# Attention bias spread over the rows by two heads at a time, the first U pair's mix read two steps later, and the values of odd softmax blocks one step later

## The chip, the cores and the metric

The kernel runs on one core of a Trainium2 chip. The time is that of one execution on the device, in microseconds; 910.57 us is the median of three runs (908.77 to 911.44). Of the core's engines the text names TensorE (PE), VectorE (DVE), ScalarE (ACT), GpSimd (POOL) and SyncE (SP), which issues most of the DMAs. Every engine works through its own list of instructions in order and waits on semaphores where it needs another's result. DMAs issued on one engine share that engine's queue.

## The reference

One block of a decoder with two token mixers side by side, for a sequence of 1024 rows and a width of 1024, all float32:

```
h      = rms_norm(x, pre_norm)
q,k,v,gate_a,u,v_b,gate_b,mg_a,mg_b = split(h @ w_in)
o_a    = sliding_window_attention(q, k, v, sinks, rel_bias)   # 16 q heads, 2 kv heads, window 128
y_a    = (o_a * silu(gate_a)) @ w_branch_a
o_b    = gelu(u) * (tril(w_s) @ layer_norm(gelu(v_b)) + b_s)  # chunks of 128, 8 groups
y_b    = (o_b * silu(gate_b)) @ w_branch_b
merged = sigmoid(mg_a) * y_a + sigmoid(mg_b) * y_b
x      = x + rms_norm(merged @ w_out, post_norm)
```

In the attention a row t sees the keys t-127 to t and one sink per head. A bias that depends on the head and on the distance between row and key alone is added to the scores before the softmax:

```
scores = einsum('bnqhgd,bnkhd->bnhgqk', qb, kb) * HEAD_DIM ** -0.5
scores = where(mask, scores + bias, NEG_INF)
m      = maximum(max(scores), sink);  p = exp(scores - m)
probs  = p / (sum(p) + exp(sink - m));  out = probs @ vb
```

## The kernel before

**Products.** A float32 operand is kept as two parts, high and low, and each product is three passes of fp32r matmuls (high by high, high by low, low by high). Over that lies a scheme of seven products for the four quarters of a result. One product is 12 matmuls of 128x512 on PE (`product`, L1079); sums of operands before it and of results behind it (`c_11`, `c_12`, `c_21`, `c22` and so on) are made by DVE, ACT and GpSimd.

**Stages.** Up to about 115 us the kernel computes the V half of the gMLP branch: tiles t of 128 rows, each with loads of x rows, a layer norm, and the spatial mix, whose result goes to `mix_d` in DRAM. Then k and v are projected. Then come 24 pairs n, each with seven steps s, one product per step. Pairs 0 to 15 alternate between Q pairs (q and `gate_a` of two heads) and M pairs (the merge gates); from pair `FIRST_U` = 16 on they are U pairs, which compute u and `gate_b` and multiply u by the mixed values. Last come three square products, by `w_branch_a`, `w_branch_b` and `w_out`, from about 672 us to the end.

**Attention beside the products.** The attention of a head pair p is laid over the products of the pairs: each step k of a head pair does a piece of it, in the middle of a product, after six of its 12 matmuls. A head pair starts every 14 steps and runs on for up to six steps into the next. It has eight blocks of 128 rows, whose scores come at k = 0, 1, 3, 4, 6, 7, 9 and 10 (`BLOCK_AT`). `blocks_at(k, lag)` gives the blocks whose turn it is, so many steps behind their scores; `even_at` and `odd_at(k, lag)` give the even ones, or the odd ones for which 3j + lag == k.

- An odd block's probabilities are transposed on PE (`transpose_p`, L1046, at k = 3j + 3), and DVE splits them into `pt_pack` (L2126, L2127).
- An even block's are transposed in small squares on DVE (L2146) and rearranged through DRAM: SP stores them at k = 3j + 2 (`prob_away`, L651, to `prob_d`) and loads them in four pieces at 3j + 3 (`prob_back`, L660, to `turned_in`). ACT and DVE split them (L1588, L2151).
- GpSimd masks the part of the previous block (`pt_prev`, L1857). PE multiplies by the values (`values`, L1067): even blocks at k = 3j + 7, odd ones at 3j + 5.
- Before that, DVE adds the bias and takes the maximum (L2137), ACT takes the exponential (L1570), DVE the reciprocal of the sum (L2117), and ACT scales (L1578).

Each engine has a function `attend(p, k)` with its part of a step, and a loop that calls it after the other work of step s of pair n; on DVE that other work is `after(n, s)`.

**The bias.** Its 384 values per head stand in DRAM (`bias_d`, 16 x 384). ACT issues one DMA in tile t = 5 that copies each head's row 128 times, to `skew_d` (16 x 128 x 384, 3 MB):

```
act.dma_start(skew_d[:, :, :], bass.AP(bias_d, 0,
    [[BIAS_ROW, N_HEADS], [0, P], [1, BIAS_ROW]])).then_inc(bias_out, 16)
```

From there `load_bias(p)` on SP reads two heads along a skewed pattern into `bias_t` (L644), for the next head pair at k = 11.

**The first U pair.** `u_mix(n)` on DVE multiplies a tile `ub` that SP loads from `mix_d` (L707) by a column of gains and adds a constant (L2172); `u_mul` (L2182) multiplies a half of u by it. In U pairs before the last they stand at steps 3 and 4. In pair 16 the last head pair's attention still runs beside them.

**x rows.** For a tile t, SP loads rows of x into `x_both` (L499, L506). DVE transposes them in squares (L1965) on the way to the h tile, of which `mv` (L1982) is a part that PE waits for (L872).

Of the kernel before, what the change touches and what calls it, by code (L numbers as in the profile page):

```python
# [5 lines left out]
P = 128  # L6
# [3 lines left out]
N_HEADS = D_MODEL // HEAD_DIM  # L10
# [9 lines left out]
HEAD_PAIRS = N_HEADS // 2  # L20
# [121 lines left out]
def build(nc, x, rel_bias, pre_norm, post_norm, w_in, sinks, sgu_ln_g, sgu_ln_b,  # L142
# [26 lines left out]
    with ExitStack() as ctx:  # L169
# [217 lines left out]
        def neg_w(blk, h):  # L387

            c = (blk % 2 * 2 + h) * SINK_W
            return neg_s[:, c:c + SINK_W]  # L390

        bmat = ub[:, 3072:4096]


# [101 lines left out]
        def _(sp):  # L496
# [140 lines left out]
                return out[0, bass.ds(t * P, P), cols]  # L637

            def load_bias(p):
                if p == 0:  # L640
                    sp.wait_ge(bias_out, 32)
                else:
                    sp.wait_ge(scores_used, 8 * p)
                sp.dma_start(bias_t[:, :].rearrange("p (h j) -> p h j", h=2),  # L644
                             bass.AP(skew_d, p * (2 * P * BIAS_ROW) + (P - 1),
                                     [[BIAS_ROW - 1, P], [P * BIAS_ROW, 2], [1, 2 * P]])).then_inc(bias_in, 16)
# [16 lines left out]
            def attend(p, k):  # L663
                for blk in even_at(k, 2):
                    prob_away(4 * p + blk // 2)
                for blk in even_at(k, 3):
                    prob_back(4 * p + blk // 2)
                if k == 11 and p + 1 < HEAD_PAIRS:
                    load_bias(p + 1)
                if k in (13, 19):  # L670
# [193 lines left out]
        def _(pe):  # L864
# [204 lines left out]
                ins.then_inc(values_ok, 1)  # L1069

            def attend(p, k):
                for blk in odd_at(k, 5) + even_at(k, 7):
                    values(p, blk)
                for blk in odd_at(k, 3):
                    transpose_p(p, blk)
                for blk in blocks_at(k, 0):
                    scores(p, blk)
# [133 lines left out]
        def _(act):  # L1211
# [107 lines left out]
            for t in range(2, NT):  # L1319
                if 2 < t < NT - 1:  # L1320
                    square_x(t + 1)
                if t == 5:
                    act.wait_ge(bias_out, 16)
                    act.dma_start(skew_d[:, :, :], bass.AP(bias_d, 0, [[BIAS_ROW, N_HEADS], [0, P], [1, BIAS_ROW]])).then_inc(bias_out, 16)
                if t == 2:
                    act.wait_ge(mix_done, 1)
                    vn_split(1)
# [596 lines left out]
        def _(dve):  # L1924
# [519 lines left out]
            def after(n, s):  # L2444
# [19 lines left out]
                if s == 3:  # L2464
                    if n and kind(n - 1) == "Q":
                        gate_mul(n - 1, 1)
                    c_22(n)
                    if kind(n) == "U" and n < PAIRS - 1:
                        u_mix(n)
                if s == 4:  # L2470
                    if n == PAIRS - 1:
                        c_11(n)
                        left_lo_square(0)
                    if kind(n) == "U":
                        u_mul(n, 0)
                    if n == PAIRS - 4:
                        right_lo_square(0)
                if s == 6:
                    if kind(n) == "Q":
                        q_lo(n, 1)  # L2480
# [120 lines left out]
```

## Time and profile before

| | us |
|---|---|
| median of three runs | 910.57 |
| lowest and highest | 908.77, 911.44 |
| the profiled execution, its own time | 908.92 |
| its span in the profile | 907.2 |
| PE busy | 894.8 |
| DVE busy | 671.5 |
| ACT busy | 500.9 |
| POOL busy | 498.2 |

The span runs from the first to the last instruction that the profile records; the execution's own time has 1.7 us around it. Shares of busy time are averages over the stages. A timeline row gives the start, the duration, the engine, the line and the operation with its output and inputs and, in brackets, how long the engine had been idle and which engine's result ended that. SPq and ACTq are the issues of DMAs on SP and ACT; their duration is that of the issue and not of the transfer. Ends of matmuls are modelled.

### The profile page before, as it was taken

The page shows a single profiled execution, that of the slowest core. Times are in us where ns is not written, and L with a number is a line of the kernel's source. Part 1 is how long each engine was busy: PE and PEld are TensorE (multiplying, and loading weights), DVE is VectorE, ACT ScalarE, POOL GpSimd, SP SyncE. Part 2 cuts the span into 40 slices and gives each one's busy share as a digit, 9 for nine tenths or more (in the row PEclk, how much of TensorE's full clock was granted, in tenths as well). Part 3 has the DMA queues.
Part 4 walks back from the last instruction along what each step waited for, and adds up shares of the span by engine and source line. Part 5 has one row for each costly group of instructions (what it writes and reads, how often), then busy time and mean ns, then how long its engine had stood idle before and what let it go on. Part 6 is the DMA issues. An engine that isn't in the chain of part 4 may idle for free.

```text
span 907.2 us, 12749 instructions
## 1 busy us (share of the span) xinstructions
PE 894.8 (99%) x4268; PEld 746.9 (82%) x4268; DVE 671.5 (74%) x1167; ACT 500.9 (55%) x982; POOL 498.2 (55%) x395
## 2 busy tenths in 40 slices
PE   9999999999999999999999989999999999999997
PEld 7888788888888888888888868888888888888886
DVE  6766695576666666757576669688689878989968
ACT  6554254775767676666767664334443434534563
POOL 3564235777787777787869636445542252043236
PEclk9999999999999999999999999999999999999999
DMA  8788764433434346534343443533289550435004
GB/s 311 194 201 241 240 209 105 136 104 86 134 88 127 95 117 163 150 105 117 102 116 103 116 146 105 186 117 123 62 292 334 185 209 1 139 114 211 1 1 185
DMA packets 170512, 130.90 MB, mean 144 GB/s; under 512 B 58552, under 2 KB 139472, under 8 KB 170320
## 3 DMA queue, kind: packets, MB, share of 16 engines
q1 hardware_dynamic: 168208, 126.66, 45.7%
q10 hardware_dynamic: 2240, 3.43, 1.2%
q8 instruction: 34, 0.56, 0.3%
q14 instruction: 30, 0.25, 0.1%
HBM read 93.87 MB, written 39.35 MB: 147 GB/s over the span
## 4 chain that ended last, share of the span: by engine, by line
PE 84%; DVE 5%; ACT 4%; issue 3%; SPq 2%; DMA 1%; POOL 0%; DVEq 0%; POOLq 0%; ACTq 0%
PE acc L1019 42%; PE acc L1200 11%; PE ps_m L1200 7%; PE ps_t L1200 7%; PE acc L872 7%; PE ps_t L1036 2%; PE acc L962 2%; PE ps_m L1067 2%; SPq L506 1%; ACT prob L1570 1%; DVE neg_s L2137 1%; DVE pt_pack L2151 1%; ACT prob L1578 1%; DVE ps_t L2134 1%; PE ps_t L1046 1%
## 5 line engine op out<-in xcount | busy, mean ns | idle before, releaser
L1019 PE MATMUL acc<-mv,w_hi 128*128 128x512 f32 x1344 | 353.8, 392 | 0.0
L1019 PEld LDWEIGHTS acc<-mv,w_hi 128*128 128x128 f32 x1344 | 244.8, 188 | 44.9
L1019 PE MATMUL acc<-mv,w_lo 128*128 128x512 f32 x672 | 182.0, 393 | 0.0
L1813 POOL TENSOR_TENSOR w_lo<-sums,w_hi 128x1024 fp32r<-128x1024 f32 x48 | 118.0, 2460 | 73.1 <-ACT w_hi L1366 48.9
L1019 PEld LDWEIGHTS acc<-mv,w_lo 128*128 128x128 f32 x672 | 126.7, 189 | 28.6
L1813 POOL TENSOR_TENSOR w_lo<-raw,w_hi 128x1024 fp32r<-128x1024 f32 (+1 forms) x48 | 95.2, 1984 | 40.1 <-ACT w_hi L1359 32.6
L1570 ACT ACTIVATE prob<-neg_s,neg_max 128x129 f32<-128x129 f32 x128 | 50.5, 396 | 89.7 <-DVE neg_max L2137 89.6
L1200 PE MATMUL acc<-right,left 128*128 128x512 f32 x432 | 98.7, 389 | 0.0
L1200 PEld LDWEIGHTS acc<-right,left 128*128 128x128 f32 x432 | 81.0, 188 | 17.2 <-DVE left L2203 0.4
L2151 DVE TENSOR_TENSOR pt_pack<-turned_in,pt_pack 128x256 fp32r<-128x256 f32 x32 | 43.6, 1362 | 42.5 <-ACT pt_pack L1588 42.5
L1857 POOL TENSOR_SCALAR_AFFINE_SELECT pt_prev<-pt_pack 128x512 fp32r<-128x512 f32 x64 | 40.8, 638 | 58.6 <-DVE pt_pack L2127 39.8
L872 PE MATMUL acc<-mv 128*128 128x512 f32 x288 | 69.3, 394 | 0.2 <-ACT mv L1233 0.2
L1200 PE MATMUL ps_t<-right,left 128*128 128x512 f32 x288 | 67.2, 389 | 0.0
L1200 PE MATMUL ps_m<-right,left 128*128 128x512 f32 x288 | 67.2, 389 | 0.0
L1200 PEld LDWEIGHTS ps_t<-right,left 128*128 128x128 f32 x288 | 54.1, 188 | 11.2
L1200 PEld LDWEIGHTS ps_m<-right,left 128*128 128x128 f32 x288 | 54.1, 188 | 11.2
L872 PEld LDWEIGHTS acc<-mv 128*128 128x128 f32 x288 | 53.2, 188 | 11.7 <-ACT mv L1233 0.4
L1578 ACT ACTIVATE prob<-prob,inv_den 128x128 f32<-128x128 f32 x128 | 44.1, 392 | 22.0 <-DVE inv_den L2117 22.0
L2137 DVE CUSTOM_DVE_ANT_0 neg_s<-ps_t,bias_t,sink_b 128x128 f32<-128x128 f32 x128 | 39.9, 350 | 4.5 <-PE ps_t L1036 2.4
L1819 POOL TENSOR_TENSOR left<-w_a,left 128x1024 fp32r<-128x1024 f32 x7 | 18.4, 2644 | 37.4 <-ACT left L1507 37.4
L1819 POOL TENSOR_TENSOR left<-s_buf,left 128x1024 fp32r<-128x1024 f32 x6 | 15.2, 2556 | 43.0 <-ACT left L1507 43.0
L1819 POOL TENSOR_TENSOR left<-w_b,left 128x1024 fp32r<-128x1024 f32 x6 | 16.4, 2751 | 38.3 <-ACT left L1507 38.3
(286 smaller groups left out, 1688.0 us busy)
## 6 DMA issues: line engine op xcount, KB each, us to landing
raw<-in_w_in SPq DMA_DIRECT2D x56, 512.0 KB, 4.5
ht_d<-sums SPq DMA_DIRECT2D x8, 512.0 KB, 4.9
mix_d<-mix_b SPq DMA_DIRECT2D x8, 512.0 KB, 4.0
prob_d<-prob SPq DMA_DIRECT2D x32, 128.0 KB, 2.2
turned_in<-prob_d SPq DMA_DIRECT2D x128, 32.0 KB, 2.2
ga_d<-gate SPq DMA_DIRECT2D x16, 256.0 KB, 4.1
tb<-tb_d SPq DMA_DIRECT2D x4, 1024.0 KB, 5.1
ub<-mix_d SPq DMA_DIRECT2D x7, 512.0 KB, 3.4
```

Of the source, the lines that this page charges most:

```text
L872: ins = nc.tensor.matmul(acc[b][:, hf * HALF:(hf + 1) * HALF], left, right, start=(m < 2), stop=(m >= 46), skip_group_check=True)
L962: ins = nc.tensor.matmul(acc[b][:, hf * HALF:(hf + 1) * HALF], (w_lo if x == 2 else w_hi)[:, w], right, start=(m < 2), stop=(m >= 46), ski ...
L1019: ins = nc.tensor.matmul(bank, (w_lo if y == 2 else w_hi)[:, left + k * P:left + (k + 1) * P], right[:, (OPW if y == 1 else 0) + k * HALF: ...
L1036: ins = nc.tensor.matmul(ps_s[:, h * 256 + lo:(h + 1) * 256], q_st[h][:, blk * P:(blk + 1) * P], kbuf[:, kc + lo:kc + 256], start=a, stop= ...
L1200: ins = nc.tensor.matmul(bank, l[:, c:c + P], r[:, (OPW if y == 1 else 0) + k * HALF:(OPW if y == 1 else 0) + (k + 1) * HALF], start=(m == ...
L1570: ins = nc.scalar.activation(prob_w(s, h, SINK_W), neg_w(blk, h), ACT.Exp, scale=-1.0, bias=neg_max[:, head(blk, h)], accum_out=row_sum[:, ...
L1578: ins = nc.scalar.activation(w, w, ACT.Copy, scale=inv_den[:, head(blk, h)])
L1813: nc.gpsimd.tensor_tensor(w_lo[:, c], src, w_hi[:, c].bitcast(f32), ALU.subtract).then_inc(wlo_ok, 1)
L1819: ins = nc.gpsimd.tensor_tensor(left[f % 2][:, OPW:2 * OPW][:, c], left_src(f // 7, ORDER[f % 7])[:, c], left[f % 2][:, c].bitcast(f32), A ...
L1857: nc.gpsimd.affine_select(out=pt_prev[blk % 2][:, :].rearrange("p (y q) -> p y q", y=4), in_=pt_pack[blk % 2][:, :].rearrange("p (y q) -> ...
L2137: ins = nc.vector.tensor_tensor_reduce(out=neg_w(blk, h)[:, 0:P], in0=ps_s[:, h * 256 + P:(h + 1) * 256], in1=bias_t[:, bias:bias + P], sc ...
L2151: nc.vector.tensor_tensor(pack[:, 256:512], turned_in[:, :], pack[:, 0:256].bitcast(f32), ALU.subtract).then_inc(ptl_ok, 1)
```

## The change

Three edits:

1. `skew(p)` gives the source and the destination of the spread of two heads. ACT issues only `skew(0)` in tile t = 5. SP issues `skew(p + 1)` at k = 7 of head pair p, seven times in all. `load_bias(p)` waits for `bias_out` of its own piece, beside `scores_used`.
2. In pair 16 alone `u_mix` and `u_mul(n, 0)` stand on DVE in step 5 and not in steps 3 and 4. The other U pairs keep them.
3. The values of odd blocks stand on PE at k = 3j + 6.

```diff
--- before.py
+++ after.py
@@ -388,6 +388,11 @@
 
             c = (blk % 2 * 2 + h) * SINK_W
             return neg_s[:, c:c + SINK_W]
+
+        def skew(p):
+
+            return (skew_d[2 * p:2 * p + 2, :, :],
+                    bass.AP(bias_d, 2 * p * BIAS_ROW, [[BIAS_ROW, 2], [0, P], [1, BIAS_ROW]]))
 
         bmat = ub[:, 3072:4096]
 
@@ -637,9 +642,8 @@
                 return out[0, bass.ds(t * P, P), cols]
 
             def load_bias(p):
-                if p == 0:
-                    sp.wait_ge(bias_out, 32)
-                else:
+                sp.wait_ge(bias_out, 32 + 16 * p)
+                if p:
                     sp.wait_ge(scores_used, 8 * p)
                 sp.dma_start(bias_t[:, :].rearrange("p (h j) -> p h j", h=2),
                              bass.AP(skew_d, p * (2 * P * BIAS_ROW) + (P - 1),
@@ -665,6 +669,8 @@
                     prob_away(4 * p + blk // 2)
                 for blk in even_at(k, 3):
                     prob_back(4 * p + blk // 2)
+                if k == 7 and p + 1 < HEAD_PAIRS:
+                    sp.dma_start(*skew(p + 1)).then_inc(bias_out, 16)
                 if k == 11 and p + 1 < HEAD_PAIRS:
                     load_bias(p + 1)
                 if k in (13, 19):
@@ -1069,7 +1075,7 @@
                 ins.then_inc(values_ok, 1)
 
             def attend(p, k):
-                for blk in odd_at(k, 5) + even_at(k, 7):
+                for blk in odd_at(k, 6) + even_at(k, 7):
                     values(p, blk)
                 for blk in odd_at(k, 3):
                     transpose_p(p, blk)
@@ -1321,7 +1327,7 @@
                     square_x(t + 1)
                 if t == 5:
                     act.wait_ge(bias_out, 16)
-                    act.dma_start(skew_d[:, :, :], bass.AP(bias_d, 0, [[BIAS_ROW, N_HEADS], [0, P], [1, BIAS_ROW]])).then_inc(bias_out, 16)
+                    act.dma_start(*skew(0)).then_inc(bias_out, 16)
                 if t == 2:
                     act.wait_ge(mix_done, 1)
                     vn_split(1)
@@ -2465,16 +2471,19 @@
                     if n and kind(n - 1) == "Q":
                         gate_mul(n - 1, 1)
                     c_22(n)
-                    if kind(n) == "U" and n < PAIRS - 1:
+                    if FIRST_U < n < PAIRS - 1:
                         u_mix(n)
                 if s == 4:
                     if n == PAIRS - 1:
                         c_11(n)
                         left_lo_square(0)
-                    if kind(n) == "U":
+                    if n > FIRST_U:
                         u_mul(n, 0)
                     if n == PAIRS - 4:
                         right_lo_square(0)
+                if s == 5 and n == FIRST_U:
+                    u_mix(n)
+                    u_mul(n, 0)
                 if s == 6:
                     if kind(n) == "Q":
                         q_lo(n, 1)
```

Lines below the new function stand five or six lines further down in the changed kernel: L651 becomes L655, L1067 becomes L1073, L2172 becomes L2178.

On SP, in the second head pair around its step 7: `raw` is the buffer of the next weight load, `ta_d` and `tb_d` are gates of M pairs. Before:

```order
L527 DMA raw<-in_w_in 128x8x128 [waits wlo_ok,sum_ok]
L651 DMA prob_d<-prob 256x1x128 [waits turn_ok]
L685 DMA tb_d<-ev 128x512 [waits mt_ok]
L660 DMA turned_in<-prob_d 32x8x32 [waits ptl_ok,prob_out]
L660 DMA turned_in<-prob_d 32x8x32 x3
L651 DMA prob_d<-prob 256x1x128 [waits turn_ok]
L644 DMA bias_t<-skew_d 128x2x256 [waits scores_used]
L660 DMA turned_in<-prob_d 32x8x32 [waits ptl_ok,prob_out]
```

And now:

```order
L532 DMA raw<-in_w_in 128x8x128 [waits wlo_ok,sum_ok]
L673 DMA skew_d<-bias_d 256x1x384
L655 DMA prob_d<-prob 256x1x128 [waits turn_ok]
L691 DMA tb_d<-ev 128x512 [waits mt_ok]
L664 DMA turned_in<-prob_d 32x8x32 [waits ptl_ok,prob_out]
L664 DMA turned_in<-prob_d 32x8x32 x3
L655 DMA prob_d<-prob 256x1x128 [waits turn_ok]
L648 DMA bias_t<-skew_d 128x2x256 [waits scores_used,bias_out]
L664 DMA turned_in<-prob_d 32x8x32 [waits ptl_ok,prob_out]
```

The spread of the next two heads stands behind a weight load and ahead of the third even block's store and loads. `load_bias` waits for it six rows further down.

On DVE, in steps 3 to 6 of pair 16, from the sum `c22` on (`ub` is the tile from `mix_d`, `bmat_in` and `mix_in0` say that its loads are there). Before:

```order
L2078 TENSOR_TENSOR c<-acc,c 128x512 [waits ev_ok]
L2172 SCALAR_TENSOR_TENSOR ub<-ub,g_col 128x1024 [waits bmat_in,mix_in0]
L2117 RECIPROCAL inv_den<-row_sum 128x2 [waits exp_ok,mm_ok]
L2151 TENSOR_TENSOR pt_pack<-turned_in,pt_pack 128x256 [waits turn_hi]
L2158 TENSOR_TENSOR o_tmp<-ps_m,o_tmp 64x256 [waits otmp_ok]
L2159 TENSOR_TENSOR o_tmp<-ps_m,o_tmp 64x256 [waits dve_own]
L2182 TENSOR_TENSOR ub<-ub,ev 128x512 [waits gu_ok]
L2126 CAST pt_pack<-ps_t 128x256 [waits values_ok,pt_done]
L2127 TENSOR_TENSOR pt_pack<-ps_t,pt_pack 128x256 [waits dve_own]
L2182 TENSOR_TENSOR ub<-ub,c 128x512 [waits gu_ok]
L2083 TENSOR_TENSOR ev<-acc,ev 128x512 [waits ev_ok,prod]
```

And now:

```order
L2084 TENSOR_TENSOR c<-acc,c 128x512 [waits ev_ok]
L2123 RECIPROCAL inv_den<-row_sum 128x2 [waits exp_ok]
L2157 TENSOR_TENSOR pt_pack<-turned_in,pt_pack 128x256 [waits turn_hi]
L2164 TENSOR_TENSOR o_tmp<-ps_m,o_tmp 64x256 [waits otmp_ok]
L2165 TENSOR_TENSOR o_tmp<-ps_m,o_tmp 64x256 [waits dve_own]
L2132 CAST pt_pack<-ps_t 128x256 [waits values_ok,pt_done]
L2133 TENSOR_TENSOR pt_pack<-ps_t,pt_pack 128x256 [waits dve_own]
L2178 SCALAR_TENSOR_TENSOR ub<-ub,g_col 128x1024 [waits bmat_in,mix_in0]
L2188 TENSOR_TENSOR ub<-ub,ev 128x512 [waits gu_ok,mm_ok]
L2188 TENSOR_TENSOR ub<-ub,c 128x512 [waits gu_ok]
L2089 TENSOR_TENSOR ev<-acc,ev 128x512 [waits ev_ok,prod]
```

The mix has moved from ahead of the reciprocal to behind the split of the last odd block, and the first multiplication stands right behind it.

On PE, in the second head pair, the values of an odd block (`ps_m` is the result, `oadd_ok` says that its bank is free) and the next transposes (`ps_t`). Before:

```order
L1067 MATMUL ps_m<-pt_pack,v_st 128x2x128 [waits oadd_ok,pt_ok]
L1067 MATMUL ps_m<-pt_pack,v_st 128x2x128
L1067 MATMUL ps_m<-pt_prev,v_st 128x2x128 x2
L1019 MATMUL acc<-mv,w_hi 128x512 x2
L1019 MATMUL acc<-mv,w_lo 128x512 [waits wlo_ok]
L1019 MATMUL acc<-mv,w_lo 128x512 x3
L1019 MATMUL acc<-mv,w_hi 128x512 [waits c22_ok,whi_ok]
L1019 MATMUL acc<-mv,w_hi 128x512 x5
L1046 MATMUL ps_t<-ident,prob 128x128 [waits ptl_ok,prob_ok]
L1046 MATMUL ps_t<-ident,prob 128x128
L1036 MATMUL ps_t<-k_hi,q_st 128x256 [waits scores_used,ql_ok]
L1036 MATMUL ps_t<-k_lo,q_st 128x256
```

And now:

```order
L1025 MATMUL acc<-mv,w_hi 128x512 x7
L1025 MATMUL acc<-mv,w_lo 128x512 [waits wlo_ok]
L1025 MATMUL acc<-mv,w_lo 128x512 x3
L1025 MATMUL acc<-mv,w_hi 128x512 [waits c22_ok,whi_ok]
L1025 MATMUL acc<-mv,w_hi 128x512 x5
L1073 MATMUL ps_m<-pt_pack,v_st 128x2x128 [waits oadd_ok,pt_ok]
L1073 MATMUL ps_m<-pt_pack,v_st 128x2x128
L1073 MATMUL ps_m<-pt_prev,v_st 128x2x128 x2
L1052 MATMUL ps_t<-ident,prob 128x128 [waits ptl_ok,prob_ok]
L1052 MATMUL ps_t<-ident,prob 128x128
L1042 MATMUL ps_t<-k_hi,q_st 128x256 [waits scores_used,ql_ok]
```

The four matmuls of the values have moved behind the rest of one product and the first half of the next, to just before the transposes of the next odd block.

## Rows read from the trace of the kernel before

**Rows 1.** Page, section 1: busy us, share of the span, instructions, by engine
```profile
PE 894.8 (99%) x4268; PEld 746.9 (82%) x4268; DVE 671.5 (74%) x1167; ACT 500.9 (55%) x982; POOL 498.2 (55%) x395
```
**Rows 2.** Waits of PE: line and what it waited for, us, times, longest us
```profile
PE ps_t L1046 <- ACT prob L1578: 3.4, 1, 3.4
...
PE acc L872 <- DVE mv L1982: 1.1, 1, 1.1
PE ps_t L1036 <- DVE neg_max L2137: 0.8, 1, 0.8
```
**Rows 3.** Timeline of PE: start us, us, operation, [idle before, releaser]
```profile
534.96 0.69 PE L1046 MATMUL ps_t<-ident,prob 128*128 128x128 f32 x2 [3.38 <-ACT prob L1578]
535.30 1.20 PE L1019 MATMUL acc<-mv,w_hi 128*128 128x512 f32 x2
...
537.88 0.85 PE L1019 MATMUL acc<-mv,w_hi 128*128 128x512 f32 x3
```
**Rows 4.** Windows: us, busy PE to POOL, PEclk, DMA share, GB/s
```profile
535.30:537.90 2.60, 2.60 (x9) 2.08 (x8) 2.14 (x5) 2.56 (x5) 0.64 (x1) 0.53 0.19 44
537.90:548.00 10.10, 10.10 (x50) 8.46 (x49) 8.49 (x10) 6.38 (x10) 7.52 (x6) 1.00 0.32 88
```
**Rows 5.** Timeline of DVE, ACT and SP's queue, 527 to 535 us
```profile
529.00 0.69 DVE L2078 TENSOR_TENSOR c<-acc,c 128x512 f32<-128x512 f32 x1 [1.01 <-ACT c L1418]
532.70 1.28 DVE L2172 SCALAR_TENSOR_TENSOR ub<-ub,g_col 128x1024 f32<-128x1024 f32 x1 [3.00 <-DMA ub<-mix_d]
...
534.22 0.69 ACT L1578 ACTIVATE prob<-prob,inv_den 128x128 f32<-128x128 f32 x2 [5.25 <-DVE inv_den L2117]
...
527.97 0.91 SPq L707 DMA_DIRECT2D ub<-mix_d  x2
```
**Rows 6.** Timeline of DVE at 93 us
```profile
93.21 1.25 DVE L1965 STREAM_TRANSPOSE sums<-x_both 128x1024 f32<-128x1024 f32 x1 [4.30 <-DMA x_both<-in_x]
```
**Rows 7.** Timeline of SP's queue, 60 to 95 us, and a DMA issue
```profile
63.95 5.75 SPq L506 DMA_DIRECT2D x_both<-in_x  x4
...
77.44 12.60 SPq L506 DMA_DIRECT2D x_both<-in_x  x4
...
skew_d<-bias_d ACTq DMA_DIRECT2D x1, 3072.0 KB, 15.8
```
**Rows 8.** DMA queues from 75 to 77 us: packets, MB, share of 16 engines
```profile
q10 hardware_dynamic: 493, 0.76, 106.7%
```
**Rows 9.** Timeline of SP's queue, second head pair
```profile
233.74 0.39 SPq L527 DMA_DIRECT2D raw<-in_w_in  x1
235.20 0.56 SPq L651 DMA_DIRECT2D prob_d<-prob  x1
...
239.71 3.38 SPq L660 DMA_DIRECT2D turned_in<-prob_d  x4
```
**Rows 10.** Landing: weight load (KB, us), the store L651, the loads L660
```profile
raw<-in_w_in SPq DMA_DIRECT2D x1, 512.0 KB, 4.3
...
DMA to landing us min/median/max: 3.2/3.2/3.2
...
DMA to landing us min/median/max: 2.0/2.2/3.0
```
**Rows 11.** Timeline of ACT, DVE and PE, 248 to 255 us
```profile
248.08 0.40 ACT L1588 ACTIVATE pt_pack<-turned_in 128x256 fp32r<-128x256 f32 x1
...
248.51 0.90 DVE L2151 TENSOR_TENSOR pt_pack<-turned_in,pt_pack 128x256 fp32r<-128x256 f32 x1 [1.07 <-ACT pt_pack L1588]
...
254.85 0.48 DVE L2151 TENSOR_TENSOR pt_pack<-turned_in,pt_pack 128x256 fp32r<-128x256 f32 x1
...
252.17 0.40 PE L1067 MATMUL ps_m<-pt_pack,v_st 128*128 128x256 f32 x2
```
**Rows 12.** Timeline of GpSimd (POOL) at 241 us, PE at 246 us
```profile
241.41 0.64 POOL L1857 TENSOR_SCALAR_AFFINE_SELECT pt_prev<-pt_pack 128x512 fp32r<-128x512 f32 x1 [1.06 <-DVE pt_pack L2127]
...
245.95 0.40 PE L1067 MATMUL ps_m<-pt_pack,v_st 128*128 128x256 f32 x2
```

## The prediction

> **What bounds the kernel now.** I read the busy shares first: TensorE (PE) is busy for 894.8 us of the 907.2 us span [rows 1], so time can be won only where PE stands still. Next come PE's own waits [rows 2]. After the start there are three: 3.38 us (3.4 in the row) for the scaled probabilities from ACT, 1.1 us for DVE's `mv`, and 0.8 us for DVE's `neg_max`. Everything else that DVE, ACT, GpSimd and the queues do lies beside matmuls. A change can give back at most these waits and what they trail behind them, while whatever it delays by more than its cover becomes a new PE wait. So for each part I ask: which of the three waits does it touch, and whose cover does it use up?
>
> **The first U pair's mix.** PE is free at 534.96 - 3.38 = 531.58 and waits until 534.96 [rows 3]. The wait has a tail: the six matmuls that follow run from 535.30 to 537.88, 2.58 us, and the granted clock of that stretch is 0.53, the lower of the two levels (1.2 GHz), after PE had stood still; the stretch after it shows 1.00 [rows 3, 4]. At the full clock the six take half of it, 1.29, so the tail is 1.29 us and the whole 3.38 + 1.29 = 4.7 us. The cause stands on DVE: it sums `c22` until 529.69, then sits 3.00 us in `u_mix` until the load of `mix_d`, issued at 527.97, has landed, and the mix takes 1.28 [rows 5]. Behind it in DVE's order is the reciprocal of the last softmax block; ACT's scaling (0.69 us) begins 0.24 us after the mix ends, and PE's transposes wait for that.
>
> With `u_mix` moved behind step 5's copies, the reciprocal follows `c22`: ACT scales from 529.69 + 0.24 = 529.93 to 530.62, 0.96 us before PE is free. The wait and its tail go. What is late next? The load lands at 532.7 as before, since its issue waits for the last mask and not for the mix. By then DVE has done the steps in front of it. It mixes until 534.0, multiplies (`u_mul`, moved with it), and its first result for PE is the sum `c_21`, which needs product 4 of this pair, two products further on. Nothing on PE waits for the mixed tile. The mix, 1.28 us, and `u_mul` are hidden by those two products; if they were not, their cost would be their own length. Term: **-4.7 us**.
>
> **The bias spread, first piece.** The wait for `mv` is the h tile of the last row block: DVE stood 4.30 us for the x rows [rows 6]. SP's four issues for these rows take 12.60 us, where the four of an earlier block took 5.75: they were held up [rows 7]. At that time the whole 3 MB spread (`skew_d`, landing after 15.8 us) filled the DMA engines: from 75 to 77 us all packets are its own, 493 of them at 106.7% of 16 engines [rows 7, 8]. The change leaves an eighth of it here, 2 heads of 16. PE needs the x rows 1.1 us sooner, out of a delay of several us. Bounds: 0 if some engines still carry as much as before, 1.1 if the way is clear. I take 0.8, nearer the upper end, since the piece leaves most engines free and ends earlier. Term: **-0.8 us**.
>
> **The bias spread, seven pieces on SP.** This is the cost. Each piece is issued on SP at step 7 of a head pair, between a 512 KB weight load and the store of the third even block's probabilities (`prob_away`). The issue itself, some 0.6 us, is hidden: SP waits for turned probabilities after it. What counts is how long a piece occupies the DMA engines, t. No row shows a spread of two heads. Ends: 15.8 / 8 = 2.0 us if it runs on all engines like the whole, 15.8 us if an eighth of the rows takes as long as all. Between them lies the rate: 493 packets in 2 us on 16 engines are 65 ns each [rows 8]. Before, 16 heads of 128 rows went over 16 engines, 128 rows each. The new source pattern begins with 2 heads, not 16. If a head stays on one engine, a piece is again 128 rows per engine: 128 x 65 ns = **8.3 us**. I take this value, since its load per engine is that of the measured spread.
>
> *The Trainium skill, "DMA: Bandwidth & Descriptors", section "Why a DMA increments its semaphore by 16 and not by 1", says that a DMA of this kind uses the largest number of engines, up to 16, that divides the outermost dimension above 1 of both patterns: here 2. No row here shows it. By it the piece has 8.3 us and the sum is the forecast; a piece spread over 16 engines would give rival 2.*
>
> Now the chain behind it, in the second pair. The weight load is issued at 233.74 and lands 4.3 later, at 238.0 [rows 9, 10]. The piece begins on its engines as that ends, about 237.5, and holds them until 237.5 + 8.3 = 245.8. The store, issued at 235.20 and landing 3.2 later, at 238.4, now lands at about 246.1. SP's four loads of turned blocks (`prob_back`) wait for that: 246.1 and not 239.71. Their issues take 2.5 us (3.38 here, one was slow), the last starts at 248.0 and lands 2.2 later [rows 10], at 250.2. ACT copies them 0.40, DVE 0.48 to 0.90 [rows 11], GpSimd 0.64 [rows 12]: ready at 251.8 to 252.3 with 0.1 for the hand-offs. PE wants them at 252.17 [rows 11]. So the cover (1.3 us in front of the loads, 3.5 us before ACT's 248.08, 2.0 us before PE) is just used up: PE waits 0 to 0.2 us, and from there one us of t costs one us in each of seven pairs. I take 0.2 x 7. The new wait of `load_bias` for its piece is covered: it stands four steps on, about 13 us, against 8.3 + 2. Behind it in SP's order stand the last block's `prob_back` loads, about 2 us late, which ACT needs at the time it has them today; its later idle time takes that up. Term: **+1.4 us**.
>
> **The values of odd blocks, one step later.** GpSimd's `pt_prev` for such a block is done at 242.05, and PE takes it at 245.95 [rows 12]: these values never wait, so a step more of room gives nothing. Nor does it cost: the four matmuls move from before one product and a half to just before the next transposes and scores, which then stand where they stood. The next odd block's copy waits for them and for the transposes directly behind, and those come last anyway. Term: **0**.
>
> **Sum**: -4.7 - 0.8 + 1.4 = -4.1 us. The profiled execution took 908.92 us; the median of the runs, 910.57, stands 1.65 above it. 908.92 - 4.1 = 904.8, and 906.5 for a median.
>
> **The rivals.** About 0.3%, 2.7 us, is what a measurement of this kernel can tell from no change.
> 1. *The pieces are too long: slower.* If a packet costs more when two engines carry all of them, or something queues in front, PE waits at the values of the third even block of seven pairs for t - 8.1 each. The gains are 5.5, so it decides from t = 8.1 + 5.5 / 7 = 8.9 us, 8% above my value. At t = 9.5 it is 7 x 1.4 = 9.8: +4.3, 914.9. For it: no cover is left in [rows 9 to 11]. Against: the 65 ns were taken with all 16 engines copying, and two should not be worse off. Chance 0.17; the end at 15.8 us (7 x 7.7) gets almost none of it.
> 2. *The pieces are short.* If they use all engines, t is 2.0 us, no chain is late, and the x rows are free: -4.7 - 1.1 = -5.8, 904.8. Against: the source pattern. Chance 0.13.
> 3. *The gain is given back: no change.* With t = 8.6 the pieces cost 3.5, or DVE, without PE's standstill to catch up in, lets PE wait about 2 us in the next U pairs: -2.0, 908.6. For it: DVE is busy at 74% [rows 1] and is given two operations later. Chance 0.25.
>
> The forecast itself has 0.45. Faster: 0.45 + 0.13 = 0.58; same 0.25; slower 0.17. The range goes from 903.5 (rival 2 and a fast set of runs) to 914.0 (t about 9.4); above it lies the far part of rival 1, near 0.1, below it 0.05.
>
> **What the profile after would show.** Right: PE's 3.4 us wait for ACT and the stretch at 0.53 gone; DVE's wait for `mix_d` at most short; seven pieces that land some 10 to 12 us after issue; `prob_away` of the third block landing after about 10 us and not 3; ACT idle before the third copy of `turned_in`. The forecast is wrong if PE shows seven waits of 1 us or more at L1073 (the values), if the pieces land after 4 us (rival 2), or if the wait for `mv` stays at 1.1 us (the term of 0.8).

## The result and the profile after

The changed kernel took 917.69 us (median of five, 914.92 to 919.85) where the kernel before took 909.84 (median of five on the same chip): a ratio of 1.0084, interval 1.0063 to 1.0105. It is slower by 7.9 us; the forecast was 906.5 with a range up to 914.0. The profiled execution took 916.38 us, 7.46 more than the one before.

The page's busy shares, to be read against [rows 1]:

```profile
PE 898.6 (98%) x4268; PEld 748.6 (82%) x4268; DVE 667.9 (73%) x1167; ACT 500.5 (55%) x982; POOL 501.1 (55%) x395
```

No engine has more instructions. PE is busy for 3.8 us more and idle for 3.6 more. PE's waits are the next view; each row names the line, what it waited for, us in all, times and the longest:

```profile
PE ps_m L1073 <- POOL pt_prev L1863: 5.9, 6, 1.6
PE ps_t L1042 <- issue: 2.0, 1, 2.0
PE acc L1096 <- DVE before L2496: 1.1, 1, 1.1
PE ps_t L1042 <- DVE neg_max L2143: 0.9, 1, 0.9
```

Against [rows 2], the wait for ACT (3.4) is gone, and so is the one for `mv` (1.1). In their place stand six waits at L1073, the values, and one at L1042 that names no engine. PE's timeline gives each its place:

```profile
251.15 0.50 PE L1073 MATMUL ps_m<-pt_pack,v_st 128*128 128x256 f32 x2 [0.29 <-POOL pt_prev L1863]
...
299.52 0.50 PE L1073 MATMUL ps_m<-pt_pack,v_st 128*128 128x256 f32 x2 [0.76 <-POOL pt_prev L1863]
...
348.44 0.51 PE L1073 MATMUL ps_m<-pt_pack,v_st 128*128 128x256 f32 x2 [1.31 <-POOL pt_prev L1863]
353.89 0.30 PE L1042 MATMUL ps_t<-k_hi,q_st 128*128 128x128 f32 x1 [1.96 <-issue]
...
400.18 0.51 PE L1073 MATMUL ps_m<-pt_pack,v_st 128*128 128x256 f32 x2 [1.05 <-POOL pt_prev L1863]
...
449.33 0.50 PE L1073 MATMUL ps_m<-pt_pack,v_st 128*128 128x256 f32 x2 [1.56 <-POOL pt_prev L1863]
...
497.89 0.50 PE L1073 MATMUL ps_m<-pt_pack,v_st 128*128 128x256 f32 x2 [0.95 <-POOL pt_prev L1863]
```

One per head pair from the second to the seventh: the third even block, the one behind a piece of the spread. The head pair's chain begins on SP's queue. The second head pair, to be read against [rows 9]:

```profile
232.37 0.39 SPq L532 DMA_DIRECT2D raw<-in_w_in  x1
232.81 0.64 SPq L673 DMA_DIRECT2D skew_d<-bias_d  x1
233.84 3.91 SPq L655 DMA_DIRECT2D prob_d<-prob  x1
237.79 0.93 SPq L691 DMA_DIRECT2D tb_d<-ev  x1
...
245.37 2.58 SPq L664 DMA_DIRECT2D turned_in<-prob_d  x4
```

The store (L655) follows the piece (L673), and the loads (L664) wait for it. They come 13.0 us after the weight load; before it was 239.71 - 233.74 = 5.97. The issue of the store alone holds SP for 3.91 us instead of 0.56. The store's landing, in this pair, and then the DMA queues from 241 to 244 us:

```profile
DMA to landing us min/median/max: 11.5/11.5/11.5
...
q1 hardware_dynamic: 98, 0.15, 13.3%
```

In those 3 us SP's queue moves 98 packets and keeps 13.3% of 16 engines busy, 2.1 of them: the piece runs on two engines. 49 packets each in 3 us are 61 ns a packet, so 128 of them take 7.8 us. By the Trainium skill, "DMA: Bandwidth & Descriptors", section "Why a DMA increments its semaphore by 16 and not by 1", the engines number the largest divisor up to 16 that the slowest dimensions of both patterns share, here 2; the trace agrees.

Where the time went is read from one more view: the start of PE's scores at step 3 of each head pair, minus the same start in the kernel before (each number is the difference of two rows of PE's timelines; the kernels' names are those of the experiments below).

| head pair | changed | pieces_alone | fourth_rows | rows96_long | pieces_on_act | rows_outermost | mix_and_values |
|---|---|---|---|---|---|---|---|
| 1st | -1.5 | -1.4 | -0.8 | -1.5 | -1.5 | -1.5 | -0.8 |
| 2nd | -1.6 | -1.4 | -0.6 | -1.7 | -1.7 | -1.6 | -0.9 |
| 3rd | -0.9 | -0.6 | 0.0 | -2.1 | -2.1 | -2.0 | -1.3 |
| 4th | +0.7 | +0.7 | +1.4 | -2.2 | -2.2 | -2.1 | -1.4 |
| 5th | +6.4 | +5.8 | +2.1 | -0.5 | -2.2 | -1.6 | -1.4 |
| 6th | +7.3 | +7.1 | +3.8 | -0.6 | -2.3 | -1.9 | -1.5 |
| 7th | +9.7 | +9.5 | +6.4 | -0.6 | -2.4 | -2.0 | -1.6 |
| 8th | +11.5 | +10.1 | +8.1 | -0.1 | -2.4 | -2.1 | -1.7 |
| its last scores | +12.1 | +10.5 | +8.8 | -0.1 | -2.5 | -2.1 | -1.7 |

The changed kernel enters the attention 1.5 us ahead (the x rows), loses 13.6 us up to its last scores, and ends 7.46 behind, so it wins 4.6 us after them (the mix).

The last column has no piece inside the attention, yet PE moves ahead by about 1 us there. That is edit 3; see values_alone below.

### The profile page after: what moved, and what is told of

It reads as the page before. It is cut to its first block, busy times and chain, and to the rows that moved or that the text cites. A ratio compares the mean times of both kernels' runs of the same rounds, so it can differ in the third digit from the quotient of the medians.

```text
span 914.6 us, 12763 instructions
## 1 busy us (share of the span) xinstructions
PE 898.6 (98%) x4268; PEld 748.6 (82%) x4268; DVE 667.9 (73%) x1167; ACT 500.5 (55%) x982; POOL 501.1 (55%) x395
## 4 chain that ended last, share of the span: by engine, by line
PE 60%; DMA 11%; DVE 9%; ACT 9%; issue 9%; SPq 2%; ACTq 0%; DVEq 0%; POOLq 0%; POOL 0%
PE acc L1025 19%; PE acc L1206 11%; PE acc L878 10%; DMA prob_d<-prob 9%; PE ps_m L1206 7%; PE ps_t L1206 7%; PE acc L968 2%; DMA turned_in<-prob_d 2%; SPq L664 2%; DVE neg_s L2143 2%; ACT prob L1584 2%; DVE gate L2109 2%; ACT prob L1576 2%; DVE ps_t L2140 1%; DVE pt_pack L2157 1%
## 5 line engine op out<-in xcount | busy, mean ns | idle before, releaser
L2157 DVE TENSOR_TENSOR pt_pack<-turned_in,pt_pack 128x256 fp32r<-128x256 f32 x32 | 38.1, 1191 | 67.3 <-ACT pt_pack L1594 67.3
L1863 POOL TENSOR_SCALAR_AFFINE_SELECT pt_prev<-pt_pack 128x512 fp32r<-128x512 f32 x64 | 44.3, 693 | 68.2 <-DVE pt_pack L2133 34.5
L1042 PE MATMUL ps_t<-k_hi,q_st 128*128 128x256 f32 (+1 forms) x128 | 35.6, 301 | 3.3 <-issue 2.0
```

What stands on the lines that cost most here:

```text
L1042: ins = nc.tensor.matmul(ps_s[:, h * 256 + lo:(h + 1) * 256], q_st[h][:, blk * P:(blk + 1) * P], kbuf[:, kc + lo:kc + 256], start=a, stop= ...
L1863: nc.gpsimd.affine_select(out=pt_prev[blk % 2][:, :].rearrange("p (y q) -> p y q", y=4), in_=pt_pack[blk % 2][:, :].rearrange("p (y q) -> ...
L2157: nc.vector.tensor_tensor(pack[:, 256:512], turned_in[:, :], pack[:, 0:256].bitcast(f32), ALU.subtract).then_inc(ptl_ok, 1)
```

## The experiments

Ratios are to the kernel before on the same chip, with their 95% interval.

| kernel | median us (range) | before | ratio |
|---|---|---|---|
| mix_alone | 904.33 (903.87 to 908.13) | 909.18 | 0.9958 (0.9944 to 0.9971) |
| values_alone | 908.70 (907.11 to 911.14) | 909.18 | 0.9993 (0.9982 to 1.0003) |
| pieces_alone | 920.08 (918.60 to 923.38) | 909.18 | 1.0125 (1.0107 to 1.0143) |
| rows_outermost | 902.12 (901.72 to 902.28) | 909.18 | 0.9920 (0.9906 to 0.9934) |
| fourth_rows | 912.80 (911.19 to 914.41) | 909.15 | 1.0036 (1.0023 to 1.0049) |
| pieces_on_act | 904.11 (901.89 to 904.76) | 909.15 | 0.9943 (0.9923 to 0.9963) |
| mix_and_values | 902.67 (902.31 to 902.78) | 909.15 | 0.9924 (0.9908 to 0.9940) |
| pieces_at_13 | 905.00 (903.85 to 905.79) | 909.15 | 0.9949 (0.9931 to 0.9967) |
| changed_again | 916.67 (916.03 to 917.11) | 909.33 | 1.0078 (1.0065 to 1.0091) |
| no_values | 917.73 (917.04 to 918.04) | 909.33 | 1.0089 (1.0076 to 1.0102) |
| rows96_long | 906.57 (904.29 to 908.15) | 909.33 | 0.9965 (0.9952 to 0.9979) |

### Each edit alone

**mix_alone**, against the kernel before:

```diff
-                    if kind(n) == "U" and n < PAIRS - 1:
+                    if FIRST_U < n < PAIRS - 1:
                         u_mix(n)
...
-                    if kind(n) == "U":
+                    if n > FIRST_U:
                         u_mul(n, 0)
...
+                if s == 5 and n == FIRST_U:
+                    u_mix(n)
+                    u_mul(n, 0)
```

> The kernel before with edit 2 alone (the mix and its first multiplication in step 5 of pair 16). Theory A (the loss comes from the pieces alone, and the mix gives what was forecast): PE's 3.38 us wait and the stretch at the lower clock are gone, 4.7 us less than before, about 905.1. Theory B (DVE catches up in PE's standstill, and loses it now): a new PE wait of about 2 us in pairs 17 to 19, about 907.

It is 4.85 us faster by the medians. The wait for ACT is gone and none has come in pairs 17 to 19: theory A. PE's waits:

```profile
PE acc L872 <- DVE mv L1982: 2.6, 1, 2.6
PE acc L1090 <- DVE before L2490: 1.1, 1, 1.1
PE ps_t L1036 <- DVE neg_max L2137: 0.8, 1, 0.8
```

The twelve runs of this kernel fall into two groups, seven at 903.9 to 904.4 us and five at 905.8 to 908.1. The profiled execution (907.66 us) is of the second and shows something else: with the spread whole, the wait for the x rows was 2.6 us here, 1.1 before [rows 2] and 0.2 in values_alone. It differs between executions.

**values_alone**, against the kernel before:

```diff
-                for blk in odd_at(k, 5) + even_at(k, 7):
+                for blk in odd_at(k, 6) + even_at(k, 7):
```

> The kernel before with edit 3 alone (the values of odd blocks at lag 6). Theory A: no change, 909.8, and the scores of the blocks at steps 4 to 7 keep their times. Theory B (the 0.3 to 0.5 us per head pair that the changed kernel loses between the scores of steps 4 and 7, ahead of the next piece, comes from the values): 2 to 3 us more, about 912.3.

Its interval holds 1: the times alone show no change. By the trace PE is 0.7 us ahead when the attention begins (the x rows, by chance) and 1.7 at its last scores, so it gains 1.0 us in between. The part between steps 4 and 7 is not lost here, so theory B falls; those losses belong to the pieces. Theory A wanted the scores at their old times, and that fails too. The gain is no chance of one trace: mix_and_values and pieces_on_act, which have edit 3 as well, gain 1.0 us in the same stretch, while mix_alone, which has not, stays 3.3 us behind the kernel before from the first scores to the last.

**pieces_alone** is the changed kernel with these two diffs undone, so that `skew`, its calls and the waits of `load_bias` are left:

```diff
-                for blk in odd_at(k, 6) + even_at(k, 7):
+                for blk in odd_at(k, 5) + even_at(k, 7):
...
-                    if FIRST_U < n < PAIRS - 1:
+                    if kind(n) == "U" and n < PAIRS - 1:
                         u_mix(n)
...
-                    if n > FIRST_U:
+                    if kind(n) == "U":
                         u_mul(n, 0)
...
-                if s == 5 and n == FIRST_U:
-                    u_mix(n)
-                    u_mul(n, 0)
```

> The kernel before with edit 1 alone (the first piece on ACT, seven on SP). Theory A: the six waits at the values, the wait for the k loads and the clock behind it stay, 1.5 us are won at the x rows: about +12, 922. Theory B (a part belongs to the values): +9.5, about 919.5.

10.9 us slower: nearer to B's number, but not for B's reason, since values_alone costs nothing. The table shows 11.9 us lost in the attention stage, 1.4 won before it. The pieces carry the whole loss.

### Why a piece is long

**rows_outermost** copies the same elements, with the pattern turned round:

```diff
-            return (skew_d[2 * p:2 * p + 2, :, :],
-                    bass.AP(bias_d, 2 * p * BIAS_ROW, [[BIAS_ROW, 2], [0, P], [1, BIAS_ROW]]))
+            return (skew_d[2 * p:2 * p + 2, :, :].rearrange("h r j -> r h j"),
+                    bass.AP(bias_d, 2 * p * BIAS_ROW, [[0, P], [BIAS_ROW, 2], [1, BIAS_ROW]]))
```

> The changed kernel with the same copy written with the 128 rows as the outermost dimension of source and destination, the heads behind them. Theory A (a piece is long because its outermost dimension is 2, so that two engines carry it): the pieces take about 2 us on all engines, the store lands after some 4 us, no wait at the values, none for k: the changed kernel less 12 to 13, about 904 to 905. Theory B (a piece of 128 rows of two heads is long whatever its order): as the changed kernel, 917.7.

902.12 us, 15.6 below the changed kernel and 7.1 below the one before: theory A, even below its number, and the lowest median of this study. SP's queue in the second head pair, and behind it the landing of that pair's store:

```profile
231.72 0.39 SPq L532 DMA_DIRECT2D raw<-in_w_in  x1
232.15 0.72 SPq L673 DMA_DIRECT2D skew_d<-bias_d  x1
233.18 0.56 SPq L655 DMA_DIRECT2D prob_d<-prob  x1
...
237.69 3.39 SPq L664 DMA_DIRECT2D turned_in<-prob_d  x4
...
DMA to landing us min/median/max: 4.5/4.5/4.5
```

The same 384 KB in the same place cost the loads nothing: 5.97 us after the weight load, as before. The piece itself landed 5.1 us after its issue. From 234 to 236 us SP's queue, with the piece and its neighbours in it, keeps all engines busy:

```profile
q1 hardware_dynamic: 885, 0.62, 106.1%
```

PE's waits in this kernel are two of about a microsecond that the kernel before has too, and one of 0.5 us at L1042. That one is for the key loads of the section on the fifth head pair below. They were issued as soon after the weight load as in the kernel before (13.1 us), but the last landed 7.3 us after its issue instead of 5.4. Why is not shown.

### What a long piece does to what stands behind it

**pieces_on_act** leaves the pieces long and issues them on ACT:

```diff
-                if k == 7 and p + 1 < HEAD_PAIRS:
-                    sp.dma_start(*skew(p + 1)).then_inc(bias_out, 16)
...
+                if k == 7 and p + 1 < HEAD_PAIRS:
+                    act.dma_start(*skew(p + 1)).then_inc(bias_out, 16)
```

> The changed kernel with the seven pieces issued on ACT at its step 7, so that they stand in another queue than the store. Theory A1 (the store waits because its packets stand behind the piece's in the same queue of two DMA engines): the store lands after 3 to 4 us, no waits at the values, 903 to 906. Theory A2 (the two engines are held, whatever the queue): as the changed kernel, 917. Between them, if the engines take turns between queues: the store lands 1 to 2 us later than before, 904 to 908.

904.11 us, and no wait at the values in the profiled execution. That one took 901.89 us; the other three took 903.93 to 904.76, and no trace shows what they had more. ACT's and SP's issues in the second head pair, then the store's landing:

```profile
232.30 0.60 ACTq L1611 DMA_DIRECT2D skew_d<-bias_d  x1
...
233.15 0.57 SPq L655 DMA_DIRECT2D prob_d<-prob  x1
...
239.77 2.83 SPq L664 DMA_DIRECT2D turned_in<-prob_d  x4
...
DMA to landing us min/median/max: 6.6/6.6/6.6
```

The store lands after 6.6 us: not 11.5, so it doesn't stand behind the whole piece, and not 3.2 as in the kernel before, so the two engines are shared. That is the case between A1 and A2, with a store that is 3.4 us later and not 1 to 2. The Trainium skill, "DMA: Bandwidth & Descriptors", section "Queues, rings and completion order", says that a DMA engine takes turns between the queues that have work for it; the 6.6 agree. The loads, 8.1 us after the weight load instead of 5.97, are late by 2.1 us, and the cover takes that. The move to ACT does two things at once, since SP also issues the store in its usual 0.57 us; the two are not told apart.

**pieces_at_13** leaves them long and on SP, but at another step:

```diff
-                if k == 7 and p + 1 < HEAD_PAIRS:
-                    sp.dma_start(*skew(p + 1)).then_inc(bias_out, 16)
+                if k == 7 and p == 0:
+                    sp.dma_start(*skew(1)).then_inc(bias_out, 16)
+                if k == 13 and p + 2 < HEAD_PAIRS:
+                    sp.dma_start(*skew(p + 2)).then_inc(bias_out, 16)
```

> The changed kernel with the same long pieces on SP, but six of them at step 13, behind the fourth even block's loads and 3 steps (some 10 us) ahead of the next store, and one head pair earlier; the second piece stays at step 7 of the first head pair. Theory A (a piece of 8 us costs only by what stands behind it): the next store comes after the piece has ended, no waits at the values: 902 to 905. Theory B (a piece costs wherever it stands, by holding two engines from every transfer, the weight loads too): over 910.

905.00 us, at the upper end of theory A, and no waits at the values. It is some 3 us above rows_outermost. By its trace 1.8 us of that are lost in the second head pair, where PE waits 0.80 us for probabilities from ACT (L1054) and 0.58 us for `neg_max` (L1044). Other transfers now stand behind the piece, which may be why; that was not tried. SP needs 3.73 us to issue the gate's store, and the second weight load follows 4.5 us after the piece:

```profile
205.60 0.63 SPq L675 DMA_DIRECT2D skew_d<-bias_d  x1
206.28 3.73 SPq L681 DMA_DIRECT2D ga_d<-gate  x1
210.11 0.39 SPq L532 DMA_DIRECT2D raw<-in_w_in  x1
```

**rows96_long** asks where the cover ends. Each piece is two DMAs, three quarters of the rows long and the rest short (`load_bias` waits for 32 + 32p):

```diff
-            return (skew_d[2 * p:2 * p + 2, :, :],
-                    bass.AP(bias_d, 2 * p * BIAS_ROW, [[BIAS_ROW, 2], [0, P], [1, BIAS_ROW]]))
+            return (skew_d[2 * p:2 * p + 2, 0:96, :],
+                    bass.AP(bias_d, 2 * p * BIAS_ROW, [[BIAS_ROW, 2], [0, 96], [1, BIAS_ROW]]))
...
+            return (skew_d[2 * p:2 * p + 2, 96:P, :].rearrange("h r j -> r h j"),
+                    bass.AP(bias_d, 2 * p * BIAS_ROW, [[0, 32], [BIAS_ROW, 2], [1, BIAS_ROW]]))
```

> The changed kernel with each of the seven pieces as two DMAs: 96 of the 128 rows with the heads outermost (three quarters of the long copy, about 6.3 us) and the other 32 with the rows outermost (short). Theory A as the prediction put it (the cover ends at 8.1 us): no loss from the pieces, 902 to 903. Theory A with the cover as the changed kernel's trace has it (7 waits of 0 to 1.6 us and a lump at the k loads at 8.4 us, so that most pairs' cover ends between 7 and 8 us): waits at the values gone or nearly so, 902 to 905. Theory B (the long pieces cost by more than the end of their chain): half of the loss or more stays, over 909.

906.57 us, 10.1 below changed_again on the same chip. All waits at the values are gone in the profiled execution, which took 904.29 us, the lowest of the seven. The store in the second head pair lands after 7.6 us (11.5 in the changed kernel), at 235.24 + 7.6 = 242.8. What is left is mainly the wait at the scores (here L1053), 1.1 us:

```profile
347.95 0.30 PE L1053 MATMUL ps_t<-k_hi,q_st 128*128 128x128 f32 x1 [1.09 <-issue]
```

So a quarter of a piece decides over some 10 us. In the six head pairs that waited at the values, the cover ends between 96 and 128 rows on two engines, 5.9 and 7.8 us at 61 ns. In the first pair it does not end even at 128, and for the loads behind the wait above it ends before 96. The mean slope is 10.1 / (7.8 - 5.9), 5 us per us. The prediction gave 7 from the end of the cover on; a part of this stretch is still covered.

### The lump at the fifth head pair

The changed kernel loses 5.7 us between the fourth and the fifth row of the table, and 0.6 to 2.4 us between any two others from the second on. The wait of 1.96 us there names no engine. SP's queue, before:

```profile
340.33 1.14 SPq L680 DMA_DIRECT2D k_hi<-k_d  x2
341.51 1.24 SPq L680 DMA_DIRECT2D k_lo<-k_d  x2
```

and in the changed kernel:

```profile
346.03 0.56 SPq L648 DMA_DIRECT2D bias_t<-skew_d  x1
346.63 1.14 SPq L686 DMA_DIRECT2D k_hi<-k_d  x2
347.81 1.24 SPq L686 DMA_DIRECT2D k_lo<-k_d  x2
```

These are the keys of the second kv head, which the scores at 353.89 are the first to need. In SP's order they stand behind the turned blocks' loads, a store and `load_bias`. They come 6.3 us later than before (18.0 us after the weight load where it was 13.1), and take some 5 us to land. **fourth_rows** turns one piece round, the one ahead of them:

```diff
+            if p == 4:
+                return (skew_d[2 * p:2 * p + 2, :, :].rearrange("h r j -> r h j"),
+                        bass.AP(bias_d, 2 * p * BIAS_ROW, [[0, P], [BIAS_ROW, 2], [1, BIAS_ROW]]))
```

> The changed kernel with the rows outermost in one piece alone, that for head pair 4. Theory A (beside the seven waits at the values there is one lump: this piece holds up SP's queue, so that the k loads of the second kv head, which stand behind it, are late, PE waits 1.96 us for them and runs 3.4 us at the lower clock behind that): 1.3 + 0.2 + 2.0 + 1.6 us or about 5 less than the changed kernel, 912 to 913; no wait of 1.96 us and no stretch at the lower clock at 355 us. Theory B (the wait of 1.96 us has another cause, such as instruction fetch): 1.5 us less, about 916, and that wait stays.

912.80, between the numbers of A. Both waits of that pair are gone, the unnamed one too: only four at the values are left. So it was the k loads.

```profile
PE ps_m L1076 <- POOL pt_prev L1866: 4.8, 4, 1.8
PE acc L1099 <- DVE before L2499: 1.1, 1, 1.1
PE ps_t L1045 <- DVE neg_max L2146: 0.9, 1, 0.9
```

Four waits are 4.8 us here. In the changed kernel the four at 299, 400, 449 and 498 us are 4.3. At the fifth head pair this kernel is 4.3 us ahead of the changed one and at the last scores 3.3: a lateness that is spared in one pair comes back in part in the next ones. I read that as PE arriving earlier at engines that did not; it was not tested.

### The values' move beside late stores

**changed_again** is the changed kernel itself; **no_values** is this:

```diff
-                for blk in odd_at(k, 6) + even_at(k, 7):
+                for blk in odd_at(k, 5) + even_at(k, 7):
```

> The changed kernel as it is, to stand beside the next two on the same chip: 915 to 920.

> The changed kernel with edit 3 undone (the values of odd blocks at lag 5 again). By the sum of the single kernels (mix_alone, values_alone, pieces_alone) it is 0.5 to 1 us slower than the changed kernel, some 918. By the traces of pieces_alone (11.9 us lost in the attention stage) and of the changed kernel (13.7 us lost) it is 1 to 2 us faster, some 916: then the values' move, worth about a microsecond where the stores are in time, costs something where they are late.

917.73 against 916.67: 1.1 us slower without the edit, what the sum of the single kernels said. The two were run on the same chip; one took 917.04 to 918.04 us and the other 916.03 to 917.11, so the ranges barely touch. By the traces no_values loses 15.0 us in the attention stage and changed_again 13.4. The reading from pieces_alone (that the move costs where stores are late) falls. pieces_alone and no_values have the same edits in that stage up to the last block and lose 11.9 and 15.0 us, so with late stores a single trace is good to some 3 us only.

**mix_and_values** is mix_alone with the diff of values_alone, and the spread whole:

```diff
-                for blk in odd_at(k, 5) + even_at(k, 7):
+                for blk in odd_at(k, 6) + even_at(k, 7):
```

> The kernel before with edits 2 and 3, the spread whole as before. Theory A: the single gains add up, -4.9 and -0.5: 903.8. What the rows-outermost kernel (902.12) has over this is the worth of a smaller first piece at the x rows less what seven short pieces cost; forecast 0.8, by the new traces 1.5 to 2, since the wait for x rows goes from 0.2 to 2.6 us between executions. Theory B (the values' move is worth its room only with late stores): 904.3.

902.67, 1.2 us below the forecast of 903.8, which as a ratio is 0.9941, just outside the interval. Its four runs are also over 1 us below the fastest of mix_alone (903.87, on another chip), as a gain of edit 3 would have it. It is 0.55 above rows_outermost, and their ratios' intervals overlap almost wholly: the division of the spread, even when written well, is worth nothing that these runs can tell.

## Why the prediction was wrong, step by step

**The U mix, -4.7: right.** mix_alone is 4.85 us faster; in the changed kernel PE wins 4.6 us behind the last scores. As written there, DVE's mix came at 545.42, without a wait, and ACT scaled 0.83 us after it ran out of work, where it had stood 5.25 [rows 5]:

```profile
545.42 1.28 DVE L2178 SCALAR_TENSOR_TENSOR ub<-ub,g_col 128x1024 f32<-128x1024 f32 x1
...
541.88 0.70 ACT L1584 ACTIVATE prob<-prob,inv_den 128x128 f32<-128x128 f32 x2 [0.83 <-DVE inv_den L2123]
```

**The first piece, -0.8: right in kind, 1.5 in the changed kernel's trace.** The wait for `mv` is gone, and PE enters the attention 1.3 to 1.6 us ahead in each kernel with the first piece on ACT, except fourth_rows (0.8). That is more than the bound of 1.1, the length of the wait. Some of it is the luck of the trace it is set against: with the spread whole, values_alone and mix_and_values enter 0.7 and 0.8 us ahead. The loads of x rows took 10.13 us to issue, 12.60 before [rows 7], 13.28 in the mix_alone execution that waited 2.6 us.

**The values, 0: wrong by 1.0 us, to the good.** The times show -0.5 alone (interval across 1) and -1.1 in the changed kernel; the traces show the 1.0 us given under values_alone. "These values never wait" is what the rows say, but from it the text took that room gives nothing. PE gains in steps too short for the list of waits (0.4 us of it in the second head pair, from step 4 to step 10); by what means is open. With this, rows_outermost is 7.1 us faster than the kernel before, where the prediction allowed 5.8 at most.

**The seven pieces, +1.4: this step failed; they cost 13.6.** That is this trace; the other three kernels with seven long pieces behind the weight load lose 11.9 to 15.0 us in the stage, and beside rows_outermost, which gains 0.6 there, it is 14.2. The length was right: 7.8 us by packets against 8.3. So, nearly, was the second pair, the one that was worked out: forecast loads 12.4 us after the weight load and a wait of 0 to 0.2 us, measured 13.0 and 0.29. There is some luck in that, since the piece was 0.5 us shorter than assumed and the loads came 0.6 us later; the forecast had no row for SP's 3.91 us at the store. Three things failed:

1. *"I take 0.2 x 7."* The cover was read in one pair of seven, which has the most of them but the first. ACT's first copy behind the loads in the second pair, and in the sixth:

```profile
249.51 0.42 ACT L1594 ACTIVATE pt_pack<-turned_in 128x256 fp32r<-128x256 f32 x1 [2.69 <-DMA turned_in<-prob_d]
...
447.70 0.42 ACT L1594 ACTIVATE pt_pack<-turned_in 128x256 fp32r<-128x256 f32 x1 [3.99 <-DMA turned_in<-prob_d]
```

   The sixth pair's weight load is issued at 429.74 and its loads at 442.80: 13.06, as in the second. Then ACT starts 4.90 us later instead of 4.14, since the loads land after up to 2.9 us and not 2.2, and PE is there 449.33 - 1.56 - 429.74 = 18.03 us after the weight load, in the second pair 251.15 - 0.29 - 232.37 = 18.49. 0.06 + 0.76 + 0.46 = 1.28 us more, a wait of 1.56. None of these is large; the chain had nothing left to take them. The six waits are 5.9 us, and each is followed by about 0.2 us more, in which the matmuls start up again: 1.2.
2. *"Behind it in SP's order stand the last block's `prob_back` loads."* That list was made for the second head pair alone. In the fourth the k loads stand there as well. They cost the wait of 1.96 us and a tail: from 354.9 to 358.4 the granted clock was 0.51, the lower level (1.2 GHz), after the two waits of 1.31 and 1.96 us, so that 3.5 us of matmuls did 1.8 us of work. Together 3.7 us. The tail is not in every execution: changed_again has none and loses 4.2 us between the same two starts instead of 5.7.

```profile
354.90:358.40 3.50, 3.50 (x10) 2.72 (x9) 3.24 (x9) 1.39 (x6) 2.51 (x3) 0.51 0.85 261
```

3. *Gaps too short for the list of waits.* 13.6 - 5.9 - 1.2 - 3.7 leaves 2.8 us, mostly in steps 4 to 7 of the head pairs from the second on, the fifth excepted, 0.1 to 0.3 us at a time. They are in pieces_alone, and not in rows_outermost and pieces_on_act; rows96_long has them in the seventh pair alone. That the long pieces on SP cause them is shown; through which engine was not tried.

**The rivals.** Rival 1 (pieces too long: slower, 0.17) is what happened, by its mechanism and at its place. Its condition was wrong: it wanted t above 8.9 us, and at 7.8 the pieces cost 13.6. It tied the case to a longer t alone, and so its chance hung on the one number that was right. The doubt belonged to the cover, which "is just used up" in the text's own words: with a slope of several us per us, a cover known to 1 us can't carry a forecast of +1.4. Rival 2 (short pieces, 904.8) is rows_outermost, 902.12.

## What to carry to other kernels

When a DMA is cut into pieces, its outermost dimension is what must stay large: two heads outermost put a copy on two engines, and the same copy with its 128 rows outermost ran on all of them and cost nothing at the values. A transfer put into a queue delays all behind it in that queue, so the list of what stands there has to be made for every place at which it is issued, down to what is needed once. Where a cover is found to be just used up, measure it in each repetition, not in one, and let the range hold the slope times the spread.

## What was not expected of the hardware

- SP itself is held: in the changed kernel the store behind a long piece took it 3.3 to 4.35 us to issue, and 0.56 behind a short one (rows_outermost; once 0.62). What the engine issues next is late as well: the gate's store in the second head pair came at 237.79, after the 3.91 us.
- A PE wait of 2 us need not cost the clock. Two executions of the same kernel: the wait of 1.96 us at the k loads was followed by 3.5 us at 0.51, the wait of 2.18 us in changed_again, behind one of 1.12 us, by none. The two stretches behind the wait there:

```profile
354.90:356.90 2.00, 2.00 (x12) 1.70 (x11) 0.80 (x2) 1.06 (x3) 1.67 (x1) 1.00 1.06 310
356.90:358.90 2.00, 2.00 (x14) 1.75 (x13) 1.93 (x8) 0.56 (x3) 1.38 (x2) 1.00 0.80 227
```

- The spread of the kernel before's own times (908.1 to 911.9 in the first set of runs) fits a collision of the whole spread with the loads of x rows, at which PE waited 0.2, 0.5, 1.1 and 2.6 us in four traces. Behind the wait of 2.6 us the granted clock was 0.64 and the next twelve matmuls took 4.60 us; behind that of 1.1 it was 1.00 and they took 3.06. rows_outermost varied by 0.6 us. mix_and_values, with the spread whole, varied by only 0.5 in four runs, so this stays a reading and is not shown.
